# Moving three modulation products from VectorE to TensorE and spacing them differently in the feed-forward loops

## The chip, the cores and the metric

The kernel runs on one core of a Trainium2 chip. The metric is the device time of one execution in microseconds. TensorE (PE) multiplies, with its weight loads (PEld) beside it; VectorE (DVE), ScalarE (ACT) and GpSimd (POOL) do elementwise work; SyncE (SP) issues most of the loads from HBM.

## The reference

A token block of 256 rows of width 1024 goes through two hybrid layers (retention, dilated attention, gated MLP, then a feed-forward part) and then through a second block (state space scan, pooling, mixture of experts). What matters here is the feed-forward part of the two layers and a small product that the second block needs and that depends on neither:

```python
# feed-forward part of each of the two layers
h = rms_norm(x, g_ffn_pre)
gate, up = jnp.split(jnp.matmul(h, w_gate_up), [FFN_HIDDEN], axis=-1)   # FFN_HIDDEN = 2816
f = jnp.matmul(jax.nn.silu(gate) * up, w_down)
# second block: one row each for the latents and the context, six parts of 1024
mod_l = jnp.split((jax.nn.silu(c) @ w_ada[i] + b_ada[i])[:, None, :], 6, axis=-1)
mod_c = jnp.split((jax.nn.silu(c_ctx) @ w_ada[i] + b_ada[i])[None, None, :], 6, axis=-1)
```

`w_ada` is 1024 x 6144 in float32, 25 MB. Only parts 0 and 1 of `mod_c` are used, since the block has one layer.

## The kernel before, in words

All five engines have programs written out by hand, each a nest of loops with semaphore waits; nothing is scheduled by a tool. Every weight unit of 1 MB passes through a ring of four slots, filled by SP. ACT writes the rounded high part of each half unit (`hi_to`, `split_r<-ring`), DVE or POOL the low part (`lo_to`), and PE multiplies each product in three passes (`mm3`).

The feed-forward part of a layer first runs over 22 column blocks m of gate and up (the up loop), then over 22 row blocks k of `w_down` (the down loop). From m = 2 on, PE makes 48 matmuls of 128x256 in block m. ACT and DVE prepare the split weights two blocks ahead. After PE has finished block m, ACT applies SiLU, DVE multiplies by the up half (`gated(m)`), ACT and POOL split the result.

The modulation product is hidden in these two up loops. It is cut into twelve units u of 512 columns, six per layer. Table `ADA_AT` gives the block m at which each begins. A unit's weights are 2 MB in two halves (buffer `AW`, `arena<-in_w_ada`, loaded by `modulation(u, h)` of SP). There is one such buffer, so the halves of the next unit are loaded only once this unit has read them. SP's list in a layer is fixed: for each unit it first issues the gate/up units that are due (`load_to`), then waits until the unit before it has released a half, then issues the half.

A unit is made in one of two ways:

- On PE (`ada_products`): after block m, 8 matmuls of 32x512 with the columns of `cs`, which wait for both halves of `AW`. DVE copies the sums from PSUM to `AD` (`products_kept`), and PE adds over the partitions in `ada_sums`, behind the matmuls of block m + 1.
- On DVE (`modulation(u, part)`): eight multiply-adds of 128x512, which sum in a PSUM bank, spread over consecutive blocks behind `gated(m)`. Only the latent row is made so. PE adds over the partitions (`ada_sums`), some blocks later.

`ada_closed(m)` of PE issues the sums that are due at block m; DVE adds the bias (`modulated_by`). Units 4, 5, 10 and 11 need one sum matmul of 128x512, the others four with two columns. For units 6 to 9 the result is laid out in another order (`in_fours`, `by_four`).

Of the kernel before, what the change touches and what calls it, by code (L numbers as in the profile page):

```python
# [290 lines left out]
def program(nc, A, out):  # L291
    st = ExitStack()
    with st:
# [111 lines left out]
        AD = [view(22400, 2, 512)[:, i, :] for i in range(2)]  # L405
# [73 lines left out]
        in_fours = lambda x: x.rearrange("t (k p) -> t p k", k=4)  # L479
        by_four = lambda x: x.rearrange("t (p k) -> t p k", k=4)  # L480
# [54 lines left out]
        slot_for = lambda r, k: expert_slots[k % (10 if r == 0 else 8)]  # L535


        ADA_AT = ({4: 0, 7: 1, 10: 2, 13: 3, 16: 4, 19: 5}, {4: 6, 7: 7, 10: 8, 13: 9, 16: 10, 19: 11})
        ADA_BY_DVE = range(4, 12)
        ada_begun = lambda l, m: [u for a, u in ADA_AT[l].items() if u not in ADA_BY_DVE and a == m]  # L540
        ada_step = lambda l, m: [(u, m - a) for a, u in ADA_AT[l].items() if u in ADA_BY_DVE and a <= m < a + 3]
        ada_ended = lambda l, m: [u for a, u in ADA_AT[l].items() if m == a + (1 if u not in ADA_BY_DVE else 3)]

        steps = [(c, d) for c in range(16) for d in range(2)]

# [4 lines left out]
        B = lambda *key: ps[:, bank_of[key], :]  # L550
# [52 lines left out]
        def tensor(t):  # L603
# [49 lines left out]
            def layer(l):  # L653
# [220 lines left out]
                def ada_products(u):  # L874

                    bk = take(("am", u), ("am", u, "kept"))
                    t.wait_ge(*at("cs"))
                    for h in range(2):
                        t.wait_ge(*at("ada_in", u, h))
                    for k in range(2):  # L880
                        for x in range(4):
                            made = t.matmul(bk[32 * x:32 * x + 32, :], cs[:, 2 * x + k, :], AW[:, x // 2, 2 * (x % 2) + k, :], k == 0, k == 1)
                    made.then_inc(*sig(s_mm, ("am", u), ("am", u, "half", 0), ("am", u, "half", 1)))
# [11 lines left out]
                def ada_closed(m):  # L895
                    for u in ada_ended(l, m):
                        ada_sums(u)
                        if u in ADA_BY_DVE:
                            drop(("am", u))
# [8 lines left out]
                for m in range(2, 22):  # L908
                    bk = take(("up", l, m), ("ff", l, m))
                    freed = [("am", u, "bank") for u, part in ada_step(l, m) if part == 0]  # L910
                    for _, u, _ in freed:
                        take(("am", u), ("am", u, "kept"), hold=True)
                    for a in range(2):
                        n = first["up", l, m][1] + a
                        wh, wl = split(n)
                        for k in range(8):
                            made = mm3(bk[:, 256 * a:256 * a + 256], wh[:, k, :], wl[:, k, :], HTH[:, k, :], HTL[:, k, :], k == 0, k == 7)
                        made.then_inc(*sig(s_mm, ("split_done", n), *([("up", l, m)] if a else freed)))
                    ada_closed(m)
                    for u in ada_begun(l, m):  # L920
                        ada_products(u)

                n0 = first["down", l][1]
                for i in range(2):
# [11 lines left out]
                for k in range(18):  # L936
                    if l and k in (12, 14):
                        turn_in("ctx", CX, k // 2 - 6)
                    down(k, 0)
                    down(k, 1).then_inc(*sig(s_mm, ("split_done", n0 + k)))  # L940
                    if k == 1:
                        ada_closed(22)
                for k in range(18, 22):
                    made = down(k, 0)
                made.then_inc(*sig(s_mm, ("dn", l, 0)))
# [460 lines left out]
            kept = list(frees)  # L1406
# [498 lines left out]
        def vector(v):  # L1905
# [14 lines left out]
            def then(made, *keys):  # L1920
                return made.then_inc(*sig(s_dve, *keys))
# [100 lines left out]
            def products_kept(u):  # L2022
                v.wait_ge(*at("am", u))
                if u >= 2:
                    v.wait_ge(*at("ada", u - 2))
                then(v.copy(AD[u % 2], B("am", u)), ("am", u, "kept"))

            def modulation(u, part):
                o, bk = AD[u % 2], B("am", u)
                row = lambda k: AW[:, k // 4, k % 4, :]  # L2030
                if part == 0:
                    v.wait_ge(*at("cs"))
                    v.wait_ge(*at("am", u, "bank"))
                for k in range(3 * part, min(3 * part + 3, 8)):
                    if k % 4 == 0:
                        v.wait_ge(*at("ada_in", u, k // 4))
                    if k:
                        v.wait_ge(*v.latest)
                    if k == 0:
                        then(v.tensor_scalar(bk, row(k), cs[:, k, 0:1], None, ALU.mult))  # L2040
                    elif k < 7:
                        then(v.stt(bk, row(k), cs[:, k, 0:1], bk, ALU.mult, ALU.add), *([("am", u, "half", 0)] if k == 3 else []))
                    else:
                        v.wait_ge(*at("ada", u - 2))
                        if u // 2 in (3, 4):
                            made = v.stt(in_fours(o), by_four(row(k)), cs[:, k, 0:1], by_four(bk), ALU.mult, ALU.add)
                        else:
                            made = v.stt(o, row(k), cs[:, k, 0:1], bk, ALU.mult, ALU.add)
                        then(made, ("am", u), ("am", u, "kept"), ("am", u, "half", 1))

            def modulated_by(u):
                bk = B("ada", u)
                v.wait_ge(*at("ada", u))
                if u // 2 in (2, 5):
                    i = 1 if u // 2 == 2 else 0
                    v.wait_ge(*at("mg_in", i))
                    then(v.tensor_tensor(MG[:, i, half(u % 2)], MG[:, i, half(u % 2)], bk, ALU.add), ("modc", u))
                    return
                o = modc[:, 4 * u:4 * u + 4, :]
                plus = u // 2 in (1, 4)  # L2060
                added_to = colT[:, 2, 4 * u:4 * u + 4]
                if u // 2 in (3, 4):
                    v.wait_ge(*at("bp_in"))
                    added_to = BP[:, 4 * u - 24:4 * u - 20]
                then(v.tensor_tensor(o, fold(bk[:, 0:8], 4), bc(added_to, 2), ALU.add), *([] if plus else [("modc", u)]))
                if plus:
                    v.wait_ge(*v.latest)
                    then(v.tensor_scalar(o, o, 1.0, None, ALU.add), ("modc", u))

            def layer(l):  # L2070
# [156 lines left out]
                for m in range(2, 22):  # L2227
                    for a in range(2):
                        lo_to(first["up", l, m][1] + a + 4)
                    gated(m)  # L2230
                    for u in ada_ended(l, m):
                        modulated_by(u)
                    for u in ada_begun(l, m):
                        products_kept(u)
                    for u, part in ada_step(l, m):
                        modulation(u, part)
                n0 = first["down", l][1]
                for k in range(18):
                    lo_to(n0 + k + 4)
                    if k == 3:  # L2240
                        for u in ada_ended(l, 22):
                            modulated_by(u)
                    if l and k in (13, 15):
                        turn_in("ctx", k // 2 - 6, 1, 0)
                lo_to(n0 + 22)
# [774 lines left out]
        def sync(y):  # L3020
# [18 lines left out]
            def load_to(u):  # L3039
                load(max(0, u - sent[0]))  # L3040
# [26 lines left out]
            for l in range(2):  # L3067
                up = [first["up", l, m][0] for m in range(22)] + [first["down", l][0] + k for k in range(11)]
                load_to(up[4])
                for q in range(2):  # L3070
                    y.wait_ge(*at("xt", 2 * l + 1, 1, q))
                y.wait_ge(*at("hl", 2 * l + 1, 1, 1))
                load_to(up[6])
                turn = list(ADA_AT[l].items())
                for x in range(len(turn) + 1):
                    for h in range(2):
                        if x:
                            m, u = turn[x - 1]
                            load_to(up[(m + 1 + h if u in ADA_BY_DVE else m) + 5])
                            y.wait_ge(*at("am", u, "half", h))  # L3080
                        if x < len(turn):
                            modulation(turn[x][1], h)
                load_to(first["z", 1, 1][0] if l == 0 else n1)
# [73 lines left out]
        @block.sync  # L3157
        def _(e):
            sync(Engine(marks, "sp", e))
# [25 lines left out]
```

## Time and profile before

| | |
|---|---|
| three runs | 1583.03, 1585.16, 1586.02 us |
| median | 1585.16 us |
| profiled execution | 1583.03 us, its span 1581.2 us |
| PE busy | 1544.4 us, 98% of the span |
| DVE, ACT, POOL busy | 877.0, 611.6, 262.8 us |
| up loop, blocks 2 to 21, layer 0 | 148.05 to 275.9 us |
| up loop, blocks 2 to 21, layer 1 | 478.85 to 598.55 us |

An engine's busy time is the union of its instructions. A timeline row merges instructions of one kind that follow without a gap: start, length, engine, line of the recording helper, names, shape, count. Each float32 matmul (not the rounded kind) leaves two records, so a unit's 8 products stand as x16. "PEclk" is the granted TensorE clock as a share of 2.4 GHz.

### The profile page before, as it was taken

What the parts mean: (1) busy time and instruction counts of PE and PEld (TensorE: products, weight loads), DVE (VectorE), ACT (ScalarE), POOL (GpSimd) and SP (SyncE); (2) the same over time, 40 slices, a digit from 0 to 9 for tenths busy, and PEclk for the clock granted to TensorE, in tenths of its full rate; (3) what the DMA queues carried; (4) which work ended last, traced back from release to release, by engine and by line L of the source; (5) the groups of instructions that cost most, each with busy time, mean ns of one, the idle gap of its engine ahead of it and who ended that gap; (6) DMA issues with size and microseconds to landing.
All of it is one profiled execution on the core that took longest, in us unless ns stands there. A gap on an engine that the chain in (4) does not pass through costs nothing.

```text
span 1581.2 us, 23840 instructions
## 1 busy us (share of the span) xinstructions
PE 1544.4 (98%) x9598; PEld 1175.7 (74%) x9598; DVE 877.0 (55%) x1441; ACT 611.6 (39%) x1111; POOL 262.8 (17%) x224
## 2 busy tenths in 40 slices
PE   8999999999999999999999999999999999999997
PEld 6889999778889998888787888998544444444542
DVE  6654447456566885678778776466433333333323
ACT  4654444345554444554457665333211111111110
POOL 2341222002322210000037662010200000000000
PEclk9999999999999999999999999999999999999998
DMA  8653998537439996423526766958999999999994
GB/s 297 215 155 96 302 285 254 200 116 252 138 96 262 314 305 218 114 81 80 159 77 196 207 192 224 282 143 319 388 415 426 420 422 425 422 422 425 421 422 197
DMA packets 249972, 410.50 MB, mean 260 GB/s; under 512 B 7685, under 2 KB 196689, under 8 KB 228480
## 3 DMA queue, kind: packets, MB, share of 16 engines
q1 hardware_dynamic: 242864, 379.09, 69.0%
q10 hardware_dynamic: 3584, 19.86, 3.2%
q0 software_dynamic: 3408, 9.95, 1.9%
q8 instruction: 79, 1.29, 0.3%
q14 instruction: 37, 0.30, 0.1%
HBM read 407.72 MB, written 1.15 MB: 259 GB/s over the span
## 4 chain that ended last, share of the span: by engine, by line
PE 83%; DMA 8%; DVE 6%; ACT 2%; issue 1%; POOL 0%; SPq 0%; DVEq 0%; ACTq 0%; POOLq 0%
PE ps L144 81%; DMA arena<-in_w_expert_up 2%; DMA arena<-in_w_expert_gate 2%; PE ps L146 2%; DVE split_r L150 2%; DVE arena L150 2%; DVE arena L154 1%; ACT split_r L148 1%; DMA cst_sb<-in_cst 1%; DMA ring<-in_w_out 1%; DMA ring<-in_w_branch_b 1%; DMA ring<-in_w_in 1%; ACT arena L148 0%; POOL stat L150 0%; DVE arena L152 0%
## 5 line engine op out<-in xcount | busy, mean ns | idle before, releaser
L144 PE MATMUL ps<-arena_r,split_r 128*128 128x256 f32 (+1 forms) x2984 | 457.4, 288 | 0.0
L150 DVE TENSOR_TENSOR split_r<-ring,split_r 128x1024 fp32r<-128x1024 f32 (+1 forms) x245 | 292.2, 1208 | 201.5 <-ACT split_r L148 194.3
L144 PEld LDWEIGHTS ps<-arena_r,split_r 128*128 128x128 f32 x2984 | 392.9, 188 | 13.3 <-issue 7.9
L148 ACT ACTIVATE split_r<-ring 128x1024 fp32r<-128x1024 f32 (+1 forms) x293 | 295.4, 1019 | 244.7 <-PE ps L144 159.2
L144 PE MATMUL ps<-split_r,arena_r 128*128 128x512 f32 (+1 forms) x1520 | 339.8, 377 | 4.6 <-issue 2.8
L144 PEld LDWEIGHTS ps<-split_r,arena_r 128*128 128x128 f32 x1520 | 274.7, 188 | 51.1 <-issue 9.4
L144 PE MATMUL ps<-arena 128*64 128x512 f32 (+8 forms) x1232 | 301.5, 470 | 3.5 <-DVE arena L160 1.7
L144 PE MATMUL ps<-hhh_r,split_r 128*128 128x256 f32 (+1 forms) x976 | 228.4, 322 | 0.0
L144 PE MATMUL ps<-ring,arena 128*64 128x512 f32 (+2 forms) x688 | 225.4, 574 | 2.6 <-DMA rows<-in_w_expert_gate 1.0
L144 PEld LDWEIGHTS ps<-arena 128*64 128x64 f32 (+2 forms) x1232 | 120.6, 150 | 112.5 <-issue 103.8
L150 DVE TENSOR_TENSOR arena<-arena,ps 128x512 f32<-128x512 f32 (+1 forms) x132 | 81.0, 640 | 195.1 <-PE ps L144 168.5
L144 PEld LDWEIGHTS ps<-hhh_r,split_r 128*128 128x128 f32 x976 | 161.6, 188 | 16.2 <-issue 3.7
L148 ACT ACTIVATE arena<-ps 128x256 f32<-128x256 f32 (+3 forms) x159 | 69.4, 447 | 254.5 <-PE ps L144 208.9
L144 PEld LDWEIGHTS ps<-ring,arena 128*64 128x64 f32 (+1 forms) x688 | 79.6, 144 | 87.6 <-issue 77.7
L150 POOL TENSOR_TENSOR split_r<-ring,split_r 128x1024 fp32r<-128x1024 f32 (+1 forms) x48 | 108.2, 2254 | 129.0 <-ACT split_r L148 100.6
L148 ACT ACTIVATE arena<-ps,modc 128x128 f32<-128x128 f32 x80 | 30.0, 454 | 195.7 <-PE ps L144 195.7
L148 ACT ACTIVATE arena_r<-arena 128x512 fp32r<-128x512 f32 (+2 forms) x96 | 50.8, 542 | 136.6 <-DVE arena L154 86.9
L144 PE MATMUL ps<-tenth,arena 128*64 128x512 f32 (+2 forms) x320 | 88.0, 466 | 3.4 <-DMA arena<-in_w_expert_gate 1.3
L154 DVE SCALAR_TENSOR_TENSOR arena<-ps,rows,arena 128x508 f32<-128x508 f32 (+4 forms) x104 | 69.7, 675 | 28.5 <-ACT arena L148 21.8
L154 DVE SCALAR_TENSOR_TENSOR arena<-ps,stat,rows 128x512 f32<-128x512 f32 x32 | 24.0, 750 | 110.5 <-PE ps L144 110.5
L150 POOL TENSOR_TENSOR arena_r<-arena,arena_r 128x256 fp32r<-128x256 f32 (+1 forms) x46 | 38.4, 837 | 252.8 <-ACT arena_r L148 252.7
L144 PEld LDWEIGHTS ps<-arena,X 128*128 128x128 f32 x576 | 67.0, 192 | 14.9 <-issue 13.3
(163 smaller groups left out, 1287.9 us busy)
## 6 DMA issues: line engine op xcount, KB each, us to landing
ring<-in_w_gate_up SPq DMA_DIRECT2D x88, 512.0 KB, 7.5
ring<-in_w_in SPq DMA_DIRECT2D x57, 512.0 KB, 5.4
arena<-in_w_ada SPq DMA_DIRECT2D x24, 1024.0 KB, 7.5
arena<-in_w_expert_gate SPq DMA_DIRECT2D x12, 2048.0 KB, 26.4
ring<-in_w_down SPq DMA_DIRECT2D x22, 1024.0 KB, 5.0
ring<-in_w_expert_up SPq DMA_DIRECT2D x11, 2048.0 KB, 24.9
ring<-in_w_expert_down SPq DMA_DIRECT2D x11, 2048.0 KB, 27.7
ring<-in_w_in SPq DMA_DIRECT2D x28, 768.0 KB, 5.4
```

Source lines behind the costliest of these rows:

```text
L144: made = e.matmul(*a, **k)
L146: made = e.transpose(*a, **k)
L148: made = e.activation(*a, **k)
L150: made = e.tensor_tensor(*a, **k)
L154: made = e.scalar_tensor_tensor(**k)
```

## The change

Units 6, 7 and 8, made by DVE before, are made by PE. The units that stay on DVE (4, 5, 9, 10, 11) take two multiply-adds in each of four blocks instead of three, three and two in three blocks. `ADA_AT` gives other starting blocks: 4, 6, 8, 10 for the PE units of layer 0 (4, 7, 10, 13 before), 4, 6, 8 for those of layer 1, and four blocks for each DVE unit. The sums of a unit that is due at "block 22" (there is one, unit 11) are issued directly behind the up loop instead of behind the second block of the down loop.

```diff
-        ADA_AT = ({4: 0, 7: 1, 10: 2, 13: 3, 16: 4, 19: 5}, {4: 6, 7: 7, 10: 8, 13: 9, 16: 10, 19: 11})
-        ADA_BY_DVE = range(4, 12)
+        ADA_AT = ({4: 0, 6: 1, 8: 2, 10: 3, 13: 4, 17: 5}, {4: 6, 6: 7, 8: 8, 10: 9, 14: 10, 18: 11})
+        ADA_BY_DVE = (4, 5, 9, 10, 11)
         ada_begun = lambda l, m: [u for a, u in ADA_AT[l].items() if u not in ADA_BY_DVE and a == m]
-        ada_step = lambda l, m: [(u, m - a) for a, u in ADA_AT[l].items() if u in ADA_BY_DVE and a <= m < a + 3]
-        ada_ended = lambda l, m: [u for a, u in ADA_AT[l].items() if m == a + (1 if u not in ADA_BY_DVE else 3)]
+        ada_step = lambda l, m: [(u, m - a) for a, u in ADA_AT[l].items() if u in ADA_BY_DVE and a <= m < a + 4]
+        ada_ended = lambda l, m: [u for a, u in ADA_AT[l].items() if m == a + (1 if u not in ADA_BY_DVE else 4)]
...
                     for u in ada_begun(l, m):
                         ada_products(u)
+                ada_closed(22)
...
                     down(k, 1).then_inc(*sig(s_mm, ("split_done", n0 + k)))
-                    if k == 1:
-                        ada_closed(22)
...
-                then(v.copy(AD[u % 2], B("am", u)), ("am", u, "kept"))
+                if u // 2 in (3, 4):
+                    then(v.copy(in_fours(AD[u % 2]), by_four(B("am", u))), ("am", u, "kept"))
+                else:
+                    then(v.copy(AD[u % 2], B("am", u)), ("am", u, "kept"))
...
-                for k in range(3 * part, min(3 * part + 3, 8)):
+                for k in range(2 * part, 2 * part + 2):
...
+                for u in ada_ended(l, 22):
+                    modulated_by(u)
                 n0 = first["down", l][1]
                 for k in range(18):
                     lo_to(n0 + k + 4)
-                    if k == 3:
-                        for u in ada_ended(l, 22):
-                            modulated_by(u)
...
-                            load_to(up[(m + 1 + h if u in ADA_BY_DVE else m) + 5])
+                            load_to(up[(m + 1 + 2 * h if u in ADA_BY_DVE else m) + 5])
```

The first place is PE in the up loop of layer 1, from its block 2. In these rows `arena_r,split_r` are block matmuls (48 per block), `arena,cs` a unit's products, `cst_sb,arena 128x2` its sums.

```order
-L144 MATMUL ps<-arena_r,split_r 128x256 x288
+L144 MATMUL ps<-arena_r,split_r 128x256 x144
+L144 MATMUL ps<-arena,cs 32x512 x8
+L144 MATMUL ps<-arena_r,split_r 128x256 x48
 L144 MATMUL ps<-cst_sb,arena 128x2 x4
```

The products of unit 6 stand behind block 4 and its sums behind block 5; before, PE had no products in this layer, and the sums stood behind block 7.

The second place is PE at the end of the same loop. `split_r,arena_r 128x512` are matmuls of the down loop (12 per block and half of the rows, so 24 for two blocks), `arena,cst_sb 128x512` the one sum of unit 10 or 11.

```order
+L144 MATMUL ps<-arena_r,split_r 128x256 x192
+L144 MATMUL ps<-arena,cst_sb 128x512
 L144 MATMUL ps<-arena_r,split_r 128x256 x144
 L144 MATMUL ps<-arena,cst_sb 128x512
-L144 MATMUL ps<-arena_r,split_r 128x256 x96
-L144 MATMUL ps<-split_r,arena_r 128x512 x24
-L144 MATMUL ps<-arena,cst_sb 128x512
-L144 MATMUL ps<-split_r,arena_r 128x512 x120
+L144 MATMUL ps<-split_r,arena_r 128x512 x144
```

The sum of unit 11 moved from behind 24 matmuls of the down loop to directly behind the last block of the up loop.

The third place is SP in layer 0. Two rows `ring<-in_w_gate_up` are one unit of the ring, `arena<-in_w_ada x2` the two halves of one modulation unit.

```order
 L170 DMA ring<-in_w_gate_up 128x8x128 x6
 L170 DMA arena<-in_w_ada 128x4x512 x2
-L170 DMA ring<-in_w_gate_up 128x8x128 x6
-L170 DMA arena<-in_w_ada 128x4x512 x2
-L170 DMA ring<-in_w_gate_up 128x8x128 x6
-L170 DMA arena<-in_w_ada 128x4x512 x2
-L170 DMA ring<-in_w_gate_up 128x8x128 x6
+L170 DMA ring<-in_w_gate_up 128x8x128 x4
+L170 DMA arena<-in_w_ada 128x4x512 x2
+L170 DMA ring<-in_w_gate_up 128x8x128 x4
+L170 DMA arena<-in_w_ada 128x4x512 x2
+L170 DMA ring<-in_w_gate_up 128x8x128 x4
```

Between two modulation units there are two ring units where there were three.

## Rows read from the trace of the kernel before

**Rows 1.** The page, its first part: busy us, share of the span, instructions.

```profile
PE 1544.4 (98%) x9598; PEld 1175.7 (74%) x9598; DVE 877.0 (55%) x1441; ACT 611.6 (39%) x1111; POOL 262.8 (17%) x224
```

**Rows 2.** Stretches of layer 0's up loop; columns as the first row names them.

```profile
core 0: us, PE busy (x) PEld busy (x) DVE busy (x) ACT busy (x) POOL busy (x), PEclk, DMA share, GB/s
165.50:185.70 20.20, 20.20 (x169) 18.63 (x168) 8.93 (x11) 7.98 (x12) 3.83 (x6) 1.00 0.99 279
185.70:205.90 20.20, 20.20 (x169) 18.64 (x168) 10.00 (x12) 9.27 (x13) 4.37 (x6) 1.00 1.09 306
```

**Rows 3.** Timeline of PE, layer 0's up loop from block 4's end.

```profile
165.49 1.93 PE L144 MATMUL ps<-arena,cs 128*32 128x512 f32 x16
167.34 6.02 PE L144 MATMUL ps<-arena_r,split_r 128*128 128x256 f32 x48
173.20 0.95 PE L144 MATMUL ps<-cst_sb,arena 128*128 128x2 f32 x8
174.01 11.77 PE L144 MATMUL ps<-arena_r,split_r 128*128 128x256 f32 x96
185.71 1.92 PE L144 MATMUL ps<-arena,cs 128*32 128x512 f32 x16
194.23 11.76 PE L144 MATMUL ps<-arena_r,split_r 128*128 128x256 f32 x96
```

**Rows 4.** Timeline of PE, layer 1's up loop.

```profile
478.85 34.80 PE L144 MATMUL ps<-arena_r,split_r 128*128 128x256 f32 x288
514.30 17.53 PE L144 MATMUL ps<-arena_r,split_r 128*128 128x256 f32 x144
532.47 17.53 PE L144 MATMUL ps<-arena_r,split_r 128*128 128x256 f32 x144
```

**Rows 5.** Single loads by SP: issue time, then us to landing; three gate/up, one modulation.

```profile
L170 SPq DMA_DIRECT2D ring<-in_w_gate_up x1: 1532/1532/1532, 169.2 to 169.2; - x1
DMA to landing us min/median/max: 6.4/6.4/6.4
...
L170 SPq DMA_DIRECT2D arena<-in_w_ada x1: 709/709/709, 172.4 to 172.4; - x1
DMA to landing us min/median/max: 11.0/11.0/11.0
...
L170 SPq DMA_DIRECT2D ring<-in_w_gate_up x1: 1843/1843/1843, 183.1 to 183.1; - x1
DMA to landing us min/median/max: 7.5/7.5/7.5
...
L170 SPq DMA_DIRECT2D ring<-in_w_gate_up x2: 1620/1685/1750, 496.2 to 497.9; - x2
DMA to landing us min/median/max: 7.3/7.4/7.5
```

**Rows 6.** Timeline of all engines at the end of layer 1's up loop.

```profile
598.55 5.79 PE L144 MATMUL ps<-split_r,arena_r 128*128 128x512 f32 x24
599.62 0.76 DVE L154 SCALAR_TENSOR_TENSOR ps<-arena,cs,ps 128x512 f32<-128x512 f32 x1
600.42 0.75 DVE L154 SCALAR_TENSOR_TENSOR arena<-arena,cs,ps 128x512 f32<-128x512 f32 x1
```

**Rows 7.** The modulation sums in DVE's instructions: ns min/median/max.

```profile
L154 DVE SCALAR_TENSOR_TENSOR arena<-arena,cs,ps x8: 748/958/1182, 259.6 to 600.4; 128x512 f32<-128x512 f32 x8
```

**Rows 8.** A stretch of the experts; columns as in rows 2.

```profile
1200.00:1300.00 100.00, 100.00 (x531) 45.13 (x528) 32.47 (x60) 12.32 (x29) 0.00 (x0) 1.00 1.01 422
```

**Rows 9.** PE: transposes at the start, the same later, and its longest later idle times.

```profile
6.00 1.97 PE L146 MATMUL ps<-cst_sb,X 128*128 128x128 f32 x8 [6.00 <-DMA cst_sb<-in_cst]
8.12 1.83 PE L146 MATMUL ps<-cst_sb,X 128*128 128x128 f32 x8
...
338.60 1.03 PE L146 MATMUL ps<-cst_sb,X 128*128 128x128 f32 x8
...
PE ps L144 <- DVE arena L150: 2.6, 3, 1.8
```

## The prediction

> **What bounds the kernel now.** I read the page first: PE is busy for 98% of the span [rows 1]. Then the stretches of the up loops: in both stretches shown PE is busy for every microsecond, at the full granted clock (1.00, so 2.4 GHz), while DVE is busy for 10 of 20 us, and the DMA engines for 0.99 and 1.09 of the time at 279 and 306 GB/s [rows 2]. So in these loops PE sets the pace, DVE has room, and the transfers have none. A busy PE row could still hide slow matmuls, so I read its timeline by start times. In layer 0, where DVE makes no modulation work, two blocks take 185.71 - 174.01 = 11.70 us, 5.85 us each [rows 3]. In layer 1, where DVE makes all of it, a stretch of three blocks with its sums repeats after 532.47 - 514.30 = 18.17 us, and six blocks ahead of it take 34.80 us, 5.8 each [rows 4]. DVE's work costs PE nothing that is seen. Moving work off DVE therefore gives nothing back, and every us put on PE counts.
>
> **Products on PE (+6.1 us).** The change adds three units of 8 matmuls. Between the start of a unit's products and the start of the next block lie 167.34 - 165.49 = 1.85 us [rows 3]. The other reading is by periods: three blocks, one set of sums and one set of products take 194.23 - 174.01 = 20.22 us [rows 3]; the same without products 18.17 us [rows 4]. The difference, 2.05 us, holds what the switch of operand kinds costs around them. So 3 x 1.85 = 5.6 at least, 3 x 2.05 = 6.15 at most; I take 6.1. Nothing lies beside them: PE has no idle time there. The sums of units 6 to 8 stay on PE, 0.81 us each (174.01 - 173.20 [rows 3]), and cost what they did. DVE loses 24 multiply-adds and gains 3 copies from PSUM, two or more of them strided. The trace has the strided multiply-add at up to 1182 ns against 748 ns [rows 7]; a strided copy may cost as much more. It ends well before the sums that wait for it, since a block of 5.85 us lies between. Zero.
>
> **Units at a distance of two blocks: the load of unit 1 (+3.5 us).** Before, three blocks lay between products, now two. The products of unit 1 need both halves of its 2 MB. SP issues these after unit 0's products and after the gate/up units that stand ahead in its list, and these are the same in both kernels up to that point (three ring units, then the two halves). Before, the second half was issued at 172.4 and landed 11.0 us later, at 183.4; the last gate/up half ahead of it, issued at 169.2, landed at 175.6 [rows 5]. Two halves thus took 7.8 us behind a full queue. The products wanted them at 185.71, so the slack was 2.3 us. Now they stand one block earlier: block 6 begins at 174.01 and ends at 174.01 + 5.85 = 179.86. PE waits 183.4 - 179.9 = 3.5 us. Behind the waiting matmul stand all of PE's blocks, and DVE's copy of unit 1 waits too, but the split of the next two blocks is already made.
>
> **The loads of units 2 and 3 (0).** Two blocks with products and sums need 2 x 5.85 + 1.85 + 0.81 = 14.4 us of PE and 4.2 MB of transfers (two ring units of 1.05 MB, one modulation unit of 2.1 MB), 291 GB/s. The transfers were seen at 279 to 306 GB/s [rows 2], so they are about even, and unit 1's stall has reset the race. The products of unit 1 end at 185.2, unit 2's are wanted at 185.2 + 5.85 + 0.81 + 5.85 = 197.7. What is ahead of its load landed at 183.1 + 7.5 = 190.6 [rows 5]; at 306 GB/s 2.1 MB take 6.9 us, at unit 1's pace 7.8, so 197.5 to 198.4. I take 7.0, and no wait (0 to 0.7). Unit 3's is behind two ring units more: 197.6 + 14.0 = 211.6, wanted at 197.7 + 1.85 + 12.5 = 212.1. No wait, up to 1.2 us at the slow pace.
>
> **The load of unit 7 in layer 1 (+1.8 us).** Block 4 ends at about 478.85 + 3 x 5.8 = 496.2 [rows 4], unit 6's products (their load is issued as before) at 498.1, and unit 7's products are wanted at 498.1 + 5.85 + 0.81 + 5.85 = 510.6. SP's list puts three ring units ahead of the load; the last half of them was issued at 497.9 and landed 7.5 us later (the larger of the pair's times [rows 5]), at 505.4. Behind it two halves take 6.9 to 7.8 us and land at 512.3 to 513.2: a wait of 1.7 to 2.6 us. I take 7.0 us, as above: a wait of 1.8. Unit 8's load is then even with its products again (0 to 1.2).
>
> **The sum of unit 11 (+2.7 us).** This is the added wait without cover. The last block of the up loop ends for PE where the down loop begins, at 598.55. DVE's last two multiply-adds of unit 11 start behind SiLU and the gate product of that block, at 599.62 and 600.42, and end at 601.17 [rows 6]. They stand there in both kernels. Before, PE ran two blocks of the down loop meanwhile. Now the sum is PE's next instruction, so PE waits 601.2 - 598.5 = 2.7 us, with the whole down loop queued behind. Layer 0 has no such place: its unit 5 begins at block 17 and is summed behind block 21, one block after DVE ended. At the other units, too, one block of 5.85 us lies between DVE's end (about 2.7 us into it) and the sum: the cover is 3 us. DVE then waits for that sum with the low part of the fourth ring half of the down loop behind it; PE needs this three row blocks later. Zero.
>
> **The sum.** 6.1 + 3.5 + 0 + 1.8 + 2.7 = 14.1 us. The profiled execution took 1583.03 us (span 1581.2), so it would take 1597.1; it was the fastest of the three shown, 2.1 below their median of 1585.16. For the median I predict 1585.2 + 14.1 = 1599.3 us.
>
> **A rule weighed.** PE was never idle for more than 1.8 us after its start and kept its clock [rows 9]. The waits here are longer, 3.5 and 2.7 us. What a slow clock costs shows at the start: 8 transposes took 1.97 us and the next 8 1.83, against 1.03 later [rows 9], so these 3.8 us cost 1.8.
> The Trainium skill (TensorE: Matmul & The Clock Gate, "HAM oscillation — how this bites in real kernels") says that an idle gap of some length between bursts of matmuls throws the array back to half of its clock, so that each wait costs more than its own length. By that rule the time would be the one of the third rival below; no row here has a wait long enough to show it.
>
> **Rivals.**
> - *The loads come in time.* Unit 1's and 7's products find their data, because the transfers ahead drain faster. Then 6.1 + 2.7 = 8.8 us remain: 1594.0. For it: the rate was up to 306 GB/s, and a few us decide. Against: up to unit 1 the two programs are the same for SP, and the landing at 183.4 is measured.
> - *The transfers fall behind.* Units 2, 3 and 8 are late as well, by the slow ends: 0.7 + 1.2 + 1.2, and unit 7 by 0.7 more, so 14.1 + 3.8 = 17.9: 1603.1. For it: the DMA engines are full. Against: each stall gives them time.
> - *The clock falls* in the waits at unit 1 and at the end of layer 1: 2 x 1.8 more, 17.7 us: 1602.9.
> - *The experts absorb it: not slower, 1585.2.* There the DMA engines are at 1.01 and 422 GB/s [rows 8]. If these loads, and not PE, set the end, and began at their old time, the delay of 14.1 us would vanish between layer 1 and the experts. It decides from the point where the first expert's load is issued: if it comes as early as before, nothing is lost. Against: it waits for a late product of the scan, behind all of SP's ring loads, and these wait for slots that PE's work releases; so it moves with PE.
>
> **How the numbers follow.** Chances: forecast 0.60, loads in time 0.12, transfers behind 0.13, clock falls 0.10, absorbed 0.05. The likeliest gives 1599.3, its own range 1597 to 1602 (5.6 against 6.1 for the products, 1.2 for the loads, and the spread of the three runs). The range of 1593.0 to 1604.5 takes in the second and third cases and the clock; only the absorbed one and a sum of several misses lie outside. What a measurement of this kernel can tell from no change is about 0.2%, 3.2 us. Every case but the absorbed one lies above 1588.4: slower 0.94, same 0.04, faster 0.02.
>
> **What would show it.** In the profile after: 64 + 48 records of `ps<-arena,cs` at 1.9 us a unit. An idle time of PE of about 3.5 us ahead of unit 1's products, released by the load of `in_w_ada`, of about 1.8 us ahead of unit 7's, none or little ahead of 2, 3 and 8. An idle time of about 2.7 us behind layer 1's up loop, released by DVE's line 154. DVE busy some 16 us less (24 x 0.76 [rows 6] less three copies). The experts' stretches as long as before, 14 us later. Wrong would be: no wait ahead of unit 1 (then the reading of SP's list fails), a shorter period of the blocks in layer 1 than the 5.8 us of before (then DVE did hold PE back), or experts that end at their old time.

## The result and the profile after

The changed kernel took 1599.71 us (median of four, 1597.26 to 1603.89), the kernel before 1585.59 us in the same comparison: a ratio of 1.0095 (95% interval 1.0069 to 1.0119), 14.1 us more. 1599.3 us had been predicted. A second session of five rounds gave the same kernel 1593.41 us (six runs, 1592.68 to 1599.19) against 1586.01, a ratio of 1.0056 (1.0043 to 1.0068), 7.4 us more. Both are slower for certain, and they differ by more than their intervals. So the first number was met partly by chance, and the two profiles have to say by what.

First PE in layer 0's up loop, the timeline of the changed kernel. It answers to [rows 3].

```profile
165.41 1.93 PE L144 MATMUL ps<-arena,cs 128*32 128x512 f32 x16
167.27 6.02 PE L144 MATMUL ps<-arena_r,split_r 128*128 128x256 f32 x48
173.12 0.95 PE L144 MATMUL ps<-cst_sb,arena 128*128 128x2 f32 x8
173.93 6.01 PE L144 MATMUL ps<-arena_r,split_r 128*128 128x256 f32 x48
183.55 3.50 PE L144 MATMUL ps<-arena,cs 128*32 128x512 f32 x16 [3.61 <-DMA arena<-in_w_ada]
186.98 6.10 PE L144 MATMUL ps<-arena_r,split_r 128*128 128x256 f32 x48
...
199.65 1.92 PE L144 MATMUL ps<-arena,cs 128*32 128x512 f32 x16
...
214.11 1.92 PE L144 MATMUL ps<-arena,cs 128*32 128x512 f32 x16
```

Unit 1's products wait 3.61 us for their load, as predicted (3.5), and units 2 and 3 wait for nothing. But the products behind the wait then take 3.50 us instead of 1.93. The stretches of the changed kernel show why (columns: us, then busy PE, PEld, DVE, ACT, POOL, then PEclk, DMA share, GB/s):

```profile
183.75:187.16 3.41, 3.41 (x17) 0.72 (x10) 0.07 (x1) 0.00 (x0) 0.00 (x0) 0.50 1.10 279
187.16:190.60 3.44, 3.44 (x29) 3.44 (x30) 1.76 (x2) 0.31 (x1) 0.00 (x0) 1.00 1.02 302
610.00:613.80 3.80, 1.30 (x10) 1.08 (x9) 2.46 (x4) 1.75 (x3) 0.73 (x1) 1.00 0.00 1
613.83:617.24 3.41, 3.41 (x8) 2.03 (x7) 1.82 (x2) 0.00 (x0) 0.72 (x1) 0.50 0.61 240
617.24:620.70 3.46, 3.46 (x16) 2.81 (x15) 0.50 (x1) 1.06 (x1) 0.00 (x0) 1.00 1.02 419
```

The granted clock is 0.50 (1.2 GHz) right behind each of the two long waits, and 1.00 again after 3.4 us of work. Between the starts of unit 1's products and of the next block lie 3.43 us (1.85 before [rows 3]): the fall cost 1.6 us. This is the third rival, and both of its places came true.

Then layer 1, the same timeline. It answers to [rows 4] and [rows 6].

```profile
483.88 17.51 PE L144 MATMUL ps<-arena_r,split_r 128*128 128x256 f32 x144
501.32 1.92 PE L144 MATMUL ps<-arena,cs 128*32 128x512 f32 x16
...
516.91 1.92 PE L144 MATMUL ps<-arena,cs 128*32 128x512 f32 x16 [1.06 <-DMA arena<-in_w_ada]
...
531.36 1.92 PE L144 MATMUL ps<-arena,cs 128*32 128x512 f32 x16
...
613.49 1.78 PE L144 MATMUL ps<-arena,cst_sb 128*128 128x512 f32 x2 [2.50 <-DVE arena L154]
```

Unit 7 waits 1.06 us (1.8 predicted), unit 8 not at all, and the sum of unit 11 waits 2.50 us for DVE (2.7 predicted).

The same rows of the changed kernel in the second session:

```profile
181.33 1.92 PE L144 MATMUL ps<-arena,cs 128*32 128x512 f32 x16 [1.35 <-DMA arena<-in_w_ada]
...
512.58 1.92 PE L144 MATMUL ps<-arena,cs 128*32 128x512 f32 x16 [0.46 <-DMA arena<-in_w_ada]
...
609.16 1.13 PE L144 MATMUL ps<-arena,cst_sb 128*128 128x512 f32 x2 [2.50 <-DVE arena L154]
```

Here unit 1 waits 1.35 us and unit 7 0.46, unit 11's sum waits 2.50 again, and no clock falls at any of the three (1.92 us for the products). The mean granted clock of the other executions points the same way: in the first session 0.993 to 0.995 in four of five executions, in the second 0.996 to 0.998 in five of six. It isn't the whole difference, since one execution of the first session took 1597.26 us at 0.997. Whether the chip has a part in it isn't known.

By stages, in us (an up loop from its first block matmul, of block 2, to the first matmul of the down loop; a down loop to the first matmul of another kind behind it; the last part begins at the first matmul behind the long wait of the routing part, 1112.0 in the kernel before; the stretches that aren't listed differ by 0.3 us at most):

| | before | after | after, second session |
|---|---|---|---|
| layer 0: up loop | 127.86 | 133.66 | 129.84 |
| layer 0: down loop | 62.70 | 62.25 | 62.25 |
| layer 1: up loop, with the wait behind it | 119.70 | 130.40 | 129.57 |
| layer 1: down loop | 64.43 | 65.35 | 63.99 |
| to the routing | 449.02 | 448.89 | 449.03 |
| routing and experts | 469.23 | 469.53 | 468.69 |

The four loops grew by 17.0 us in the first profile and by 11.0 in the second. Products (6.1), unit 1's wait, unit 7's wait and unit 11's wait make 13.3 and 10.4 of it; two falls of the clock at 1.6 make 3.2 more in the first. About half a us is left in each, 0.27 of it at the place of unit 11's sum (see the experiment on that sum). The sum of unit 5 now also stands in the up loop of layer 0 instead of its down loop, which moves about 0.45 us from the second row to the first.

### The profile page after: what moved, and what is told of

It is laid out like the page before. It is cut to its first block, busy times and chain, and to the rows that moved or that the text cites. A ratio compares the mean times of both kernels' runs of the same rounds, so it can differ in the third digit from the quotient of the medians.

```text
span 1598.0 us, 23908 instructions
## 1 busy us (share of the span) xinstructions
PE 1555.6 (97%) x9646; PEld 1179.4 (74%) x9646; DVE 861.3 (54%) x1420; ACT 612.2 (38%) x1111; POOL 262.0 (16%) x224
## 4 chain that ended last, share of the span: by engine, by line
PE 82%; DMA 9%; DVE 5%; ACT 2%; issue 1%; SPq 1%; POOL 0%; ACTq 0%; DVEq 0%; POOLq 0%
PE ps L144 80%; DMA arena<-in_w_expert_up 2%; DMA arena<-in_w_expert_gate 2%; PE ps L146 2%; DVE arena L150 1%; DMA arena<-in_w_ada 1%; DVE split_r L150 1%; DMA ring<-in_w_in 1%; ACT split_r L148 1%; DVE arena L154 1%; DMA ring<-in_w_branch_a 1%; DMA cst_sb<-in_cst 1%; SPq L170 1%; DMA ring<-in_w_gate_up 0%; ACT arena L148 0%
## 5 line engine op out<-in xcount | busy, mean ns | idle before, releaser
L144 PEld LDWEIGHTS ps<-arena,X 128*128 128x128 f32 x576 | 67.7, 193 | 14.1 <-issue 12.5
```

The source lines that it names most:

```text
L144: made = e.matmul(*a, **k)
```

## The experiments

**The three products alone**

```diff
-        ADA_BY_DVE = range(4, 12)
+        ADA_BY_DVE = (4, 5, 9, 10, 11)
```
(and the copy in the changed kernel's form; `ADA_AT` as before)

> The kernel before with one part of the change alone: units 6, 7 and 8 are made by PE, at the old blocks 4, 7 and 10; spacing, DVE's steps and the place of the last sum are as before. My theory: three products at 2.05 us each, 6.1 us more (+0.39%), no wait for a load, since three blocks lie between, and no fall of the clock. Rival, DVE relieved gives something back: less than 5.6 us more, and layer 1's up loop less than 5.6 us longer.

1589.01 us against 1585.86, ratio 1.0021 (1.0012 to 1.003): 3.2 us more. Yet by the profile layer 1's up loop takes 125.82 us in place of 119.70, 6.12 more, and no other stage is longer. The timeline of this kernel:

```profile
495.77 1.92 PE L144 MATMUL ps<-arena,cs 128*32 128x512 f32 x16
497.62 6.02 PE L144 MATMUL ps<-arena_r,split_r 128*128 128x256 f32 x48
503.48 0.95 PE L144 MATMUL ps<-cst_sb,arena 128*128 128x2 f32 x8
504.29 11.76 PE L144 MATMUL ps<-arena_r,split_r 128*128 128x256 f32 x96
515.98 1.92 PE L144 MATMUL ps<-arena,cs 128*32 128x512 f32 x16
```

The period is now layer 0's, 524.50 - 504.29 = 20.21 us (20.22 in [rows 3]) in place of 18.17. The term of 6.1 us is right, and nothing was given back in the loop. Why the medians show only half of it is taken up with the routing below.

**The spacing of layer 0 alone**

```diff
-ADA_AT = ({4: 0, 7: 1, 10: 2, 13: 3, 16: 4, 19: 5}, ...
+ADA_AT = ({4: 0, 6: 1, 8: 2, 10: 3, 16: 4, 19: 5}, ...
```

> The kernel before with one part alone: the PE units 1, 2 and 3 of layer 0 stand behind blocks 6, 8 and 10 (before 7, 10, 13). Theory: PE waits 3.6 us for unit 1's load, none for units 2 and 3; if the clock falls in that wait as in the changed kernel's trace, 1.6 us more, 5.2 in all. Rival, the wait is made up later in the loop: the down loop of layer 0 then begins less than 3 us late. Rival, the clock does not fall: 3.6 us.

1588.63 us (twelve runs from 1582.97 to 1593.09), ratio 1.0015 (1.0004 to 1.0026). The profile refutes the 3.6 us as a fixed number:

```profile
180.63 1.92 PE L144 MATMUL ps<-arena,cs 128*32 128x512 f32 x16 [0.51 <-DMA arena<-in_w_ada]
182.48 6.02 PE L144 MATMUL ps<-arena_r,split_r 128*128 128x256 f32 x48
```

The wait is real and in its place, but 0.51 us long, and the loop is 0.59 us longer. The load was issued at 170.7 and landed 9.8 us later, at 180.5. SP's list up to this load is the same in all kernels but two, so I can compare its landing over nine other profiles: 183.4 (before), 183.4 (after), 181.2, 184.0, 181.5, 182.4, 183.3, 181.2, 182.7. It moves by 3.5 us between executions. Most of that stands already in the issue, here in SP's rows of this kernel and then of the changed one:

```profile
155.05 13.80 SPq L170 DMA_DIRECT2D ring<-in_w_gate_up  x6
```
```profile
155.43 15.63 SPq L170 DMA_DIRECT2D ring<-in_w_gate_up  x6
```

The six gate/up halves ahead take SP 13.8 to 15.9 us to issue, the second half of unit 1 is issued at 170.7 to 172.8 over the ten profiles, and it lands 9.8 to 11.8 us later. Where PE asks at 179.9, the wait is 0.5 to 4 us, 2.5 on the mean of the ten. The times of this kernel spread over 10 us, those of the first experiment over 2.7.

**The sum of unit 11 alone**

```diff
+                if l:
+                    ada_closed(22)
                 n0 = first["down", l][1]
...
-                    if k == 1:
+                    if k == 1 and l == 0:
                         ada_closed(22)
```
(DVE's `modulated_by` moved in the same way)

> The kernel before with one part alone: the sum of unit 11 stands directly behind layer 1's up loop instead of behind two blocks of the down loop. Theory: PE waits 2.5 to 2.7 us for DVE's last two multiply-adds; with a fall of the clock behind it 1.7 us more, 4.2 to 4.4 in all. Rival, the fall in the changed kernel's trace at this place has another cause or depends on where the wait falls: 2.6 us alone.

1589.14 us, ratio 1.0024 (1.0015 to 1.0032), 3.3 us more. The timeline, and the stretch behind the wait:

```profile
600.77 2.08 PE L144 MATMUL ps<-arena,cst_sb 128*128 128x512 f32 x2 [2.50 <-DVE arena L154]
```
```profile
600.77:604.20 3.43, 3.43 (x6) 2.12 (x7) 1.32 (x2) 0.00 (x0) 0.73 (x1) 0.50 0.64 209
```

The wait is 2.50 us and the clock is at 0.50 behind it. The two loops of layer 1 together take 188.52 us, 4.39 more than before, as expected with a fall; by the times it is 3.3. How the 4.39 divide is seen in two later kernels that differ in the place of this sum alone and whose clock did not fall there: with the sum directly behind the up loop (the experiment on SP's list) the two loops take 193.03 us, with the sum in its old place (both waits taken away) 190.26. So the place costs 2.77 us, 2.50 of them wait, and the fall the other 1.6, as at unit 1.

**PE kept busy in the waits**

```diff
+                    if u == 1:
+                        fill(bk, 12)
                     for h in range(2):
                         t.wait_ge(*at("ada_in", u, h))
...
                     bk = take(("ada", u), ("modc", u))
+                    if u == 11:
+                        fill(bk, 8)
```

> The changed kernel, with PE kept busy in its two long waits by matmuls whose results are overwritten: 12 of 32x512 ahead of unit 1's products (about 2.8 of 3.6 us), 8 ahead of unit 11's sum (about 1.85 of 2.5 us). Theory, the clock falls because PE is idle there: no fall at these places, the first product set takes 1.9 us instead of 3.5, and the kernel is 3.3 us faster than the changed one (about 1596.4). Rival, the slow clock is no part of the loss, or the fillers cost more than they save: no gain, 1599.7 or more.

1598.60 us, ratio 1.0081 (1.0068 to 1.0094). Its timeline:

```profile
179.88 2.78 PE L144 MATMUL ps<-cst_sb,cs 128*32 128x512 f32 x24
182.49 1.90 PE L144 MATMUL ps<-arena,cs 128*32 128x512 f32 x16
...
607.40 1.92 PE L144 MATMUL ps<-cst_sb,cs 128*32 128x512 f32 x16
609.98 1.12 PE L144 MATMUL ps<-arena,cst_sb 128*128 128x512 f32 x2 [0.65 <-DVE arena L154]
```

No clock fell at either place, and the up loop of layer 0 takes 130.90 us against 133.66. The gain of 3.3 us in the time did not come: 1.1 us, not told apart. One reason is in the rows: the load landed at 181.5 this time, so the fillers ran 1.0 us too long. The other is a fall of 6.8 us at 1125.9, in the routing, and 472.3 us for the last stage against 469.5 (which had a fall of 3.4 us there). And against the unfilled kernel of the second session, whose clock did not fall at these places, the filled one is slower by 5.2 us (measured in different sessions and on different chips). As a remedy it failed; that the slow clock needs the idle time agrees with it, but one profile without a fall doesn't show it, since the second session had none either.

**SP's list**

```diff
-load_to(up[(m + 1 + 2 * h if u in ADA_BY_DVE else m) + 5])
+load_to(up[m + 1 + 2 * h + 5 if u in ADA_BY_DVE else m + 4])
```

> The changed kernel with one line of SP's list different: the halves of units 1, 2, 3 (layer 0) and 7, 8 and the one behind them (layer 1) are issued one ring unit earlier. Theory, the wait at unit 1 is a load that queues behind the ring units ahead of it in SP's list: with 1.05 MB less ahead it lands about 3.4 us earlier, at about 180, so a wait of 0 to 0.5 us at unit 1 and none at unit 7, no fall of the clock there, and layer 0's up loop of 128.3 to 128.9 us where the changed kernel has 133.7; the whole about 1596 to 1597. Rival, the rate of the transfers and not the place in the list decides: the ring units that come later then hold PE, and the loop stays at 131 or more.

1593.04 us (five runs, 1591.52 to 1593.72), ratio 1.0043 (1.003 to 1.0057). SP's timeline and then PE's:

```profile
154.96 9.97 SPq L170 DMA_DIRECT2D ring<-in_w_gate_up  x4
167.42 0.92 SPq L170 DMA_DIRECT2D arena<-in_w_ada  x2
168.50 11.47 SPq L170 DMA_DIRECT2D ring<-in_w_gate_up  x4
```
```profile
173.96 6.01 PE L144 MATMUL ps<-arena_r,split_r 128*128 128x256 f32 x48
179.89 1.92 PE L144 MATMUL ps<-arena,cs 128*32 128x512 f32 x16
...
606.96 1.13 PE L144 MATMUL ps<-arena,cst_sb 128*128 128x512 f32 x2 [2.50 <-DVE arena L154]
```

With one ring unit less ahead, the halves are issued at 167.4, as soon as unit 0 is done, and land at 178.4. Nobody waits for a load, in either layer, and layer 0's up loop takes 128.33 us. The ring units that come later hold nothing up. So the wait at unit 1 is one of queueing order, and the rival falls. The whole took 3 us less than the 1596 to 1597 expected, and its time isn't told apart from the changed kernel's second session (1593.41); the gain is shown by the up loop of layer 0 alone, 128.33 us against 133.66 and 129.84. The wait of 2.50 us for unit 11 is still there, and here no clock fell behind it.

**The routing part filled, in the kernel before**

The kernel before already puts filler matmuls (`turn_over`) into its routing part and still has waits of 1.77 and 0.93 us there.

```diff
-                turn_over(1, 14)
+                turn_over(1, 21)
...
-                turn_over(2, 5)
+                turn_over(2, 8)
```

> The kernel before with 7 and 3 more filler matmuls in the two waits of the routing part (0.24 us each; waits of 1.77 and 0.93 us). Theory, a random fall of the clock at these waits makes the executions differ: three of the six profiles so far have it and their last stretch is 3 to 4 us longer. So without it: the fastest runs stay at about 1583, the median comes down from 1585.9 to 1583.5 to 1584.5 and the spread shrinks. Rival, the spread has another cause, such as the transfers of the experts: median and spread as before.

1582.15 us (eleven runs, 1581.45 to 1584.23) against 1585.95 (1583.3 to 1589.51), ratio 0.9975 (0.9966 to 0.9984): 3.8 us faster, more than expected, and the spread shrank from 6.2 to 2.8 us. This is faster than both kernels of the comparison. (My expectation counted the profiles wrongly: four of six had a fall there, three of them with the longer stretch.) What a long fall does is seen in two timelines of kernels without the fillers, first the spacing experiment, then the kernel before:

```profile
1113.21 0.63 PE L144 MATMUL ps<-arena,cst_sb 128*128 128x64 f32 x4 [1.76 <-DVE arena L150]
...
1115.96 6.55 PE L144 MATMUL ps<-arena,X 128*128 128x128 f32 x32 [0.91 <-DVE arena L152]
```
```profile
1112.00 0.63 PE L144 MATMUL ps<-arena,cst_sb 128*128 128x64 f32 x4 [1.77 <-DVE arena L150]
...
1114.76 3.81 PE L144 MATMUL ps<-arena,X 128*128 128x128 f32 x32 [0.93 <-DVE arena L152]
```

The same waits, and 32 matmuls take 6.55 or 3.81 us. Of the ten profiles without the fillers seven have a fall there. In all seven it begins 0.3 to 1.7 us behind the end of the wait of 1.77 us and before the wait of 0.93 begins, so the second wait has no part in it. Two of the falls last 6.8 us and make the routing 2.6 and 2.7 us longer, five last 3.4 us and cost 0.5 to 0.7. Here is one of each, the spacing experiment and then the kernel with both waits taken away, whose slow filler matmuls use up the second wait:

```profile
1114.88:1121.70 6.82, 5.91 (x29) 5.77 (x28) 2.28 (x8) 0.00 (x0) 0.46 (x1) 0.50 1.01 426
```
```profile
1118.24:1121.65 3.41, 3.41 (x17) 3.29 (x17) 1.93 (x11) 0.00 (x0) 0.00 (x0) 0.50 1.02 431
```
```profile
1118.19 2.44 PE L144 MATMUL ps<-cst_sb 128*128 128x128 f32 x10
1120.49 4.37 PE L144 MATMUL ps<-arena,X 128*128 128x128 f32 x32
```

With the fillers, in this kernel:

```profile
1111.47 0.63 PE L144 MATMUL ps<-arena,cst_sb 128*128 128x64 f32 x4 [0.21 <-DVE arena L150]
...
1114.23 3.81 PE L144 MATMUL ps<-arena,X 128*128 128x128 f32 x32 [0.26 <-DVE arena L152]
```

That the fillers help is shown by the times; that the falls are the whole of it is not. Over the ten profiles the falls of the routing cost 0.8 us on the mean. The rival of the expectation, the transfers of the experts, has a part in the spread: PE's last wait for an expert load (`arena<-in_w_expert_gate`) is 2.4 to 2.5 us in four profiles, among them the three with the longer stretch, and 1.0 to 1.3 in the other eight. The mean granted clock of each execution says the same. Of the 26 executions of the kernel before that this comparison has 19 stand at 0.995 or 0.996, where its two profiles without a fall stand at 0.997, and none of the eleven with fillers stands below 0.997: most of its executions have a fall. (One of 3.4 us at half the clock lowers the mean by 0.001.) But the 17 at 0.996 have a median of 1585.9 us and the seven at 0.997 one of 1585.5, both far above 1582.15; only the two at 0.995 (1589.4 and 1589.5) stand out. So 2 to 3 of the 3.8 us have no cause that these runs show.

**The three products, with the routing filled**

Both edits together: the diff of the first experiment and the one above.

> The three units on PE at the old blocks (as in the first experiment) with the same fillers in the routing part. The first experiment gave 6.1 us more in layer 1's up loop by its profile, but only 3.2 us more by the medians. Theory, the products cost 6.1 us and the rest is the random fall in the routing: this kernel is 5.5 to 6.5 us slower than the kernel before with the same fillers. Rival, a part of the 6.1 us is given back later, where the experts' transfers set the pace: 3 to 4 us slower than that kernel.

1587.77 us (eleven runs, 1586.8 to 1589.68), 5.6 us more than the 1582.15 of the same session with the same fillers. With the fillers in both kernels the products cost by the times nearly what the profile says (6.1). Nothing is given back in the experts: their stage takes 468.16 and 468.19 us in these two. The fillers gain more in the kernel before (3.8 us by the medians) than in the one with the products (about 1.2, from two sessions). Why isn't shown.

**Both waits taken away**

The changed kernel with SP's list of the experiment above, and `ada_closed(22)` and `modulated_by` back in their old places in the down loop.

> The changed kernel with both waits taken away: SP's list as in the experiment on the list, and the sum of unit 11 behind two blocks of the down loop again. What stays is the three units on PE. Theory: as slow as the first experiment with the products alone, 3 to 6 us more than the kernel before, so 1589 to 1592. Rival, the four-block steps of DVE or the two-block distance cost something by themselves: 1594 or more.

1589.23 us, ratio 1.0024 (1.0015 to 1.0034), as the products alone (1589.01). Its up loop of layer 1 takes 125.82 us to the hundredth as there, and layer 0's takes 128.33 us, where the 0.47 more than before are the sum of unit 5, which stood in the down loop. So four-block steps of DVE and the two-block distance cost nothing by themselves. What the change costs beyond its products lies in its waits.

**The two kernels once more**

> The changed kernel once more, for a second profile and more times. Theory, the moment at which unit 1's load lands differs between executions by 3.5 us (180.5 to 184.0 in the six profiles with this list), so the wait ahead of unit 1's products is 0.5 to 4 us here and the times spread over 1595 to 1604 as in the first four; the wait ahead of unit 11's sum is 2.5 us again, to within 0.1, since both sides of it are fixed; median 1597 to 1601. Rival, the wait at unit 1 is 3.6 us in every execution of this kernel: 3.4 to 3.8 again.

This is the second session told above: 1593.41 us, outside the 1597 to 1601 that I gave the median. The waits came as the theory says (1.35 at unit 1, 2.50 at unit 11), the spread did not.

> The kernel before once more, one profile. Theory, the slow clock in the routing part comes to this kernel too in most of its executions: a fall of the granted clock near 1115 and a last stretch of about 472 us in place of 469.2, and about 1586. Rival, it belongs to the changed orders alone: no fall and 469 us again. The load of unit 1 lands at 180 to 184 and nobody waits for it.

1584.45 us, one run. No fall in the routing, last stage 469.61 us, the load of unit 1 landed at 182.7 and nobody waited. So the expectation of a fall missed. With the first profile, both of this kernel's profiles have none, and both executions (1583.03, 1584.45) lie below its median. That most of its executions have one rests on their mean granted clock (told at the fillers), not on a profile. This stage was 469.61 us without a fall because PE waited 2.36 us for an expert load.

## Why the prediction was right, and where only by luck

- **DVE has room, PE sets the pace: right.** The busy time of DVE fell by 15.7 us (877.0 to 861.3), and the products alone made the loop longer by their full price.
- **Products, +6.1: right.** 6.12 by the stage. The upper of the two readings holds, by periods: the 1.85 us between starts leave out 0.2 us per unit. That these are the switch of operand kinds, as predicted, no run shows. The strided copies took 1.10 us each (the row below, by shape, layer 1) and held nobody.

```profile
L160 DVE COPY arena<-ps 128x512 f32<-128x512 f32 x3 | 3.3, 1100 | 3.2 <-PE ps L144 3.2
```

- **Unit 1's load, +3.5: the mechanism right, the size a draw.** The step that failed is "the landing at 183.4 is measured". It was measured once. Over ten executions with the same list it is 180.5 to 184.0, and the issue ahead of it 170.7 to 172.8, so the term is 0.5 to 4 us. The profiled execution after it had 3.61.
- **Units 2, 3 and 8, 0: right.** No wait in any profile of the changed kernel.
- **Unit 7, +1.8: too large.** 1.06 and 0.46 us. The term rested on the same kind of single landing.
- **Unit 11's sum, +2.7: right.** 2.50 us in four profiles of four. Both ends of this wait hang on the same event, the end of the last block, and so it doesn't vary. The 0.2 us are in the PE row, whose start of the next matmul I took for the end of the block. The place as a whole costs 2.77 us without a fall.
- **The clock: a rival that came in.** It had 0.10. In the up loops of the first profile it added 3.2 us, in those of the second nothing. Behind unit 11's wait of 2.50 us it fell in two profiles of four; behind unit 1's wait of 3.61 it fell, behind 1.35 and 0.51 it didn't. The rule of the Trainium skill (TensorE: Matmul & The Clock Gate, "HAM oscillation — how this bites in real kernels") thus holds here in its direction; but behind the routing wait of 1.77 us, which the prediction took for harmless [rows 9], the clock fell too, in seven of ten profiles, and behind the wait of 2.4 to 2.5 us for an expert load in one of four.
- **The experts absorb nothing: right.** Their stage takes 468.2 to 469.6 us in nine profiles of twelve, whether PE comes there 0 or 17 us later, and 472.0 to 472.5 in the other three, which have 6.8 us of slow clock in it in all and a wait of 2.5 us for an expert load where most have 1.0. PE's arrival decides neither.
- **The sum.** Without the clock the steps gave 14.1; measured they are 13.3 in one execution and 10.4 in another, and by the times 14.1 in one session and 7.4 in the other. The direction was certain; the first session's agreement to 0.1 us was not earned. The range (1593.0 to 1604.5) holds both medians.

## What to carry to other kernels

Before a term of a sum is taken from one landing of a load in a full queue, ask how much that landing moves; a wait whose two ends hang on one event is as good as fixed, one against a load is a range, and the issuer's rows show how much of the range is there before the load is even issued. An item may be brought forward in an instruction stream only together with the loads that it needs in the issuer's list: moving the load by one unit took that wait away. And on PE count a short wait as its length plus a chance of the slow clock behind it.

## What the runs showed of the hardware

The granted clock fell to 0.50 behind idle times of PE as short as 1.77 us (seven of ten executions, all of them before the next idle time began) and 2.50 us (two of four), and not in the others, with the same rows ahead. A fall that the trace shows for 3.4 us cost 1.6 us where PE was busy throughout, and 0.5 to 0.7 us in the routing, where a wait behind it took up the rest; one of 6.8 us cost 2.7 us in the 32 matmuls behind it. Ten filler matmuls of 0.24 us, in a place where PE had nothing to do, made the whole kernel 3.8 us faster, of which the falls explain only a part. A load of 1 MB behind six others was issued at 170.7 to 172.8 us and landed at 180.5 to 184.0, in ten executions with the same list.
